# Index units ahead of the convolution units, index dots inside the convolution units, and the 24-row tile of k, q and v on four column groups

## The reference

```python
z = rms_norm(x, g) @ w_in            # 1024 -> q 512, k 512, v 512, ga 512, qi 256, wi 8, ki 32, ub 256, gb 256, cv 256, cg 256, gc 256
q = partial_rope(rms_norm(q per head, q_g)); k = partial_rope(rms_norm(k per head, k_g))     # 8 heads x 64
qi, ki = partial_rope(qi), partial_rope(ki)                                                # 8 index heads x 32
uc = cv * sigmoid(cg)
# A: the keys of each query are chosen by an indexer
sc  = sum_h wi[h] * relu(qi[h] . ki)           # "index dots", masked by position
idx = top_k(sc, L/4);  att = softmax(q . k[idx]) @ v[idx]
# B: causal pooling of ub, windows 2/4/8/16, per-group linear map
# C: depthwise causal convolution of uc, width 31 ("taps"), LayerNorm, swish
y = concat(att * silu(ga), pool * silu(gb), conv * silu(gc));  x = x + y @ w_out
```

## Time and profile before

| | us |
|---|---|
| median of 3 runs (all: 747.38, 752.42, 752.99) | 752.42 |
| profiled execution, its own time | 746.28 |
| its span | 745.0 |
| PE busy | 702.3 (94%) |
| DVE busy | 523.2 (70%) |
| ACT busy | 331.2 (44%) |
| POOL busy | 300.3 (40%) |

### The profile page before, as it was taken

The page is one execution under the profiler, slowest core; times in us unless marked ns, Lnnn a source line. Parts: engine busy times, 40 slices in busy tenths (PEclk is TensorE's granted clock), DMA queues, the critical chain, the costliest instruction groups (busy, mean ns, idle before and its releaser), DMA issues.

```text
span 745.0 us, 13366 instructions
## 1 busy us (share of the span) xinstructions
PE 702.3 (94%) x4690; PEld 567.3 (76%) x4690; DVE 523.2 (70%) x1320; ACT 331.2 (44%) x850; POOL 300.3 (40%) x445
## 2 busy tenths in 40 slices
PE   5899999999889999998999999999988799999998
PEld 5897756578777777776999866666878688777797
DVE  3538888899977977435663898989997777822232
ACT  5525646533947333334132555543485643332212
POOL 1013698942848710011120459895376763000000
PEclk9999999999989999999999999999999899999999
DMA  5543040314232536014025304031522244501203
GB/s 195 160 137 118 17 128 30 114 35 143 58 87 60 179 136 227 1 58 139 21 92 153 126 4 142 30 88 46 157 58 61 83 151 167 170 1 57 96 22 112
DMA packets 54979, 71.90 MB, mean 97 GB/s; under 512 B 12977, under 2 KB 30585, under 8 KB 54881
## 3 DMA queue, kind: packets, MB, share of 16 engines
q1 hardware_dynamic: 54802, 70.96, 30.0%
q10 hardware_dynamic: 111, 0.08, 0.0%
HBM read 64.05 MB, written 7.61 MB: 96 GB/s over the span
## 4 chain that ended last, share of the span: by engine, by line
PE 70%; DVE 21%; ACT 3%; issue 2%; DMA 2%; POOL 1%; SPq 0%; ACTq 0%; DVEq 0%; POOLq 0%
PE R L1273 16%; PE R L1260 6%; PE R L1244 6%; PE R L1262 6%; PE R L1261 6%; PE R L1245 6%; PE R L1246 6%; DVE bias L1715 5%; DVE small L1713 5%; PE R L1409 4%; PE A L1360 3%; PE A L1213 2%; PE A L1438 2%; DVE W_r L1614 2%; PE R L1213 1%
## 5 line engine op out<-in xcount | busy, mean ns | idle before, releaser
L1260 PE MATMUL R<-x_hi,W_r 128*128 128x268 f32 x448 | 137.7, 307 | 5.9 <-DVE bufA L1614 3.3
L1262 PE MATMUL R<-x_hi,W_r 128*128 128x268 f32 x448 | 133.3, 297 | 0.0
L1261 PE MATMUL R<-x_lo,W_r 128*128 128x268 f32 x448 | 133.0, 297 | 0.0
L1244 PE MATMUL R<-W_r,x_hi 128*128 128x512 f32 (+3 forms) x320 | 123.0, 385 | 3.3 <-DVE W_r L1614 3.3
L1273 PE MATMUL R<-yT,W 128*128 128x268 f32 (+2 forms) x768 | 124.2, 318 | 1.0 <-DVE gt L1882 1.0
L1273 PEld LDWEIGHTS R<-yT,W 128*128 128x128 f32 x768 | 106.9, 190 | 16.8 <-issue 6.2
L1245 PE MATMUL R<-W_r,x_hi 128*128 128x512 f32 (+3 forms) x320 | 118.4, 370 | 0.0
L1246 PE MATMUL R<-W_r,x_lo 128*128 128x512 f32 (+3 forms) x320 | 118.1, 369 | 0.0
L823 POOL TENSOR_TENSOR W_r<-W,W_r 128x256 fp32r<-128x256 f32 x112 | 79.4, 742 | 53.1 <-ACT W_r L940 52.3
L1260 PEld LDWEIGHTS R<-x_hi,W_r 128*128 128x128 f32 x448 | 89.5, 200 | 14.5 <-issue 8.5
L1261 PEld LDWEIGHTS R<-x_lo,W_r 128*128 128x128 f32 x448 | 89.9, 201 | 0.0
(11 more groups left out here) (259 smaller groups left out, 1219.7 us busy)
## 6 DMA issues: line engine op xcount, KB each, us to landing
W<-in_w_in SPq DMA_DIRECT2D x52, 512.0 KB, 4.7
KV<-in_cache_k SPq DMA_DIRECT2D x32, 256.0 KB, 3.0
W<-in_w_out SPq DMA_DIRECT2D x8, 1024.0 KB, 6.6
KV<-in_cache_v SPq DMA_DIRECT2D x32, 256.0 KB, 3.9
ubx<-qkv_rows SPq DMA_DIRECT2D x16, 256.0 KB, 3.5
W<-in_w_in SPq DMA_DIRECT2D x8, 296.0 KB, 3.5
out_new_k_prompt<-kz SPq DMA_DIRECT2D x8, 256.0 KB, 2.2
out_new_v_prompt<-V SPq DMA_DIRECT2D x8, 256.0 KB
```

The lines of the kernel that those rows point to most:

```text
L1244: pe.matmul(out, x_hi[:, kc, rows], hi, start=(kc == 0), stop=False)
L1260: pe.matmul(out, hi[:, cols], x_hi[:, kc, toks], start=(kc == 0), stop=False)
L1261: pe.matmul(out, hi[:, cols], x_lo[:, kc, toks], start=False, stop=False)
L1262: m = pe.matmul(out, lo[:, cols], x_hi[:, kc, toks], start=False, stop=(kc == KC - 1))
```

## The change

Five things move or change, in both layers:
- The idx units come first (tiles 1, 2, 0, 3, 4), then the state turns, then the conv units. The idx turns stand behind the first three conv units, and all 40 index dots stand inside the last five conv units, a pair behind every second `kc`. The dots have four PSUM banks instead of two. DVE gathers eight pieces ahead of the evacuation of each of these conv units.
- In the k and q loops of PE no dots are left. DVE's loops hold three taps per tile (four in the last) and two selects per tile.
- Tile 0 of k, q and v is made by `unit_first`: x is put together again for these 24 rows (`x24`, one POOL row), and plain float32 products with both weight parts run on four column groups of 128 output columns, 64 matmuls of 24 x 128 instead of 24 of 24 x 512. ACT evacuates tile 0 in four pieces (k and q: four copies and four squares; v: four copies).
- The weights of the idx units are the ones loaded and split first. For layer 1 the first two of these four loads are split at step "ahead" (four ACT and four DVE rows of 296 columns instead of eight of 256), the other two behind the value products, ahead of the last eight output units (ACT) and between the evacuations of these (DVE).
- Some ACT and DVE weight splits and SP's stores of the index keys move with them.

The diff, cut:

```diff
-EARLY = (CONV_ORDER
-         + [("idx", i, 0) for i in range(NT)]
+IDX_ORDER = (1, 2, 0, 3, 4)
...
             first = slice(XCOL[0], XCOL[0] + ROWS_P[0])
+            x24_s.did(pool.tensor_tensor(x24[:, :, :], x_hi[:, :, first].bitcast(F32), x_lo[:, :, first].bitcast(F32), ALU.add))
...
+                if i == 0:
+                    for j in range(4):
+                        copy(kz[0:r, n % 3, 128 * j:128 * j + 128], R[32 * j:32 * j + r, bank(u), 0:128], rinv[0:r, 0:1])
...
+            for n in range(5):
+                for p in range(8 * n, 8 * n + 8):
+                    relu(p)
...
+            def unit_first(u, name):
+
+                k, g = open_unit(u), G[name]
+                for kc, hi, lo, more in chunks(g):
+                    for w in (hi, lo):
+                        for j in range(4):
+                            m = pe.matmul(R[32 * j:32 * j + ROWS_P[0], k, 0:128], x24[:, kc, :], w[:, 128 * j:128 * j + 128].bitcast(F32),
+                                          start=(kc == 0 and w is hi), stop=(kc == KC - 1 and w is lo), skip_group_check=True)
...
             def unit_fm(u, name, col):
...
+                    if u in DOTS_OF and kc % 2 == 1:
+                        dots(DOTS_OF[u] + kc - 1)
...
+            turns_behind = {("conv", 0, 0): (1, 2), ("conv", 1, 0): (0, 3), ("conv", 0, 1): (4,)}
+            for u in CONV_ORDER:
+                unit_fm(u, ("cv", "cg")[u[1] // 2], 128 * (u[1] % 2))
...
             for i in range(NT):
-                unit_tm(("k", i, 0), "k", 4 * i)
+                if i == 0:
+                    unit_first(("k", 0, 0), "k")
+                else:
+                    unit_tm(("k", i, 0), "k")
                 if i >= 2:
                     kq_turn(i - 2)
...
             for u in CONV_ORDER:
+                if u in DOTS_OF:
+                    for p in range(DOTS_OF[u], DOTS_OF[u] + 8):
+                        gather(p)
...
             for i in range(NT):
-                for x in range(0, IX_K, 2):
-                    gather(p)
-                    gather(p + 1)
-                    p += 2
-                    for _ in range(TAPS_K[i] // 2 if x else (TAPS_K[i] + 1) // 2):
-                        tap(j)
-                        j += 1
+                for x in range(TAPS_K[i]):
+                    tap(j)
+                    j += 1
+                between(2)
                 kq_sum(i)
...
                 if n == SX["ahead"] + 1 and l + 1 < DEPTH:
-                    dve.wait_ge(*next_hi.at(4 * AHEAD))
-                    for m in range(AHEAD):
-                        split_rest(dve, l + 1, m, next_lo)
+                    for n_hi in range(4):
+                        dve.wait_ge(*next_hi.at(n_hi + 1))
+                        split_rest(dve, l + 1, n_hi // 2, n_hi % 2, next_lo)
```

More of the change, by code:

```diff
@@ L416, in first_sync @@
                 x_load(i)
-            first_w(0)
-            first_w(1)
+            for m in range(AHEAD):
+                first_w(m)
             x_load(3)
@@ L708, in sync_layer @@
             row_z.did(sp.dma_start(z_dram, zi[0:8, 0, :]))
+            for m in range(10, 14):
+                w_load(m)
             def k_store(i):
@@ L844, in rotate @@
                 return ta, tb
-            for i in range(NT):
+            for i in IDX_ORDER:
                 r = ROWS_P[i]
@@ L1061, in scalar_layer @@
             for i in range(NT):
[L1062 to L1066, removed]
+                if i in (1, 2):
+                    scale_block(15 + i)
                 kq_evac(NT + i)
@@ L1307, in spread, with x_ready, dots, idx_turn @@
                 stage.did(m)
+            def x_ready(i):
+                if l == 0:
+                    pe.wait_ge(*pre_kept.at(2 * i + 2))
+                elif i == 0:
+                    pe.wait_ge(*xd_s.at(0))
+                elif i < 3:
+                    pe.wait_ge(*res_s.at(3 * KC * i - 9 * KC))
+            def dots(first):
+                if first == 0:
+                    pe.wait_ge(*idxk_s.at(NT))
+                    pe.wait_ge(*row_s.at(3))
+                elif first >= 4:
+                    pe.wait_ge(*acc_s.at(first - 2))
+                for p in (first, first + 1):
+                    i, h, lo, hi = PIECES[p]
+                    b = 32 * (h % 4)
+                    ix_s.did(pe.matmul(A[0:ROWS[i], p % 4, 0:hi - lo], qkT[b:b + 32, h // 4, START[i]:START[i] + ROWS[i]],
+                                       qkT[b:b + 32, 2, lo:hi], start=True, stop=True))
+            def idx_turn(i):
+                n = IDX_NTH[i] - 1
+                pe.wait_ge(*idxz_s.at(n + 1))
+                if n >= 2:
+                    pe.wait_ge(*idxk_s.at(n - 1))
+                for j in range(3):
+                    m = turn(A[:, n % 2, 128 * j:128 * j + ROWS_P[i]], zi[0:ROWS_P[i], i, 128 * j:128 * j + 128], ROWS_P[i])
+                idxt_s.did(m)
+            for i in IDX_ORDER:
+                x_ready(i)
+                if l == 0 and i == 0:
+                    pe.wait_ge(*pre_par_k.at(DEPTH))
+                unit_tm(("idx", i, 0), "idx")
+                if l == 0 and i == 1:
+                    first_params(pe)
+                    first_turn(pe, 3)
+                    first_turn(pe, 4)
+                if l and i == 2:
+                    pe.wait_ge(*sa_s.at(0))
+                    for x in range(NT):
+                        m = pe.matmul(A[0:SR, 3, x:x + 1], row[:, XCOL[x]:XCOL[x] + SR], ones[:, 0:1], start=True, stop=True)
+                    stats_s.did(m)
             pe.wait_ge(*diag_s.at(NT))
```

304 lines of the change are left out of this document (140 added, 164 removed).

## The result

The changed kernel takes **776.81 us** (median; 775.74 to 777.84) against 751.46 of before in the same comparison: ratio 1.0346, interval 1.0301 to 1.0391, 25.4 us slower. The forecast was 767, within 750 to 780. The direction and the place are as forecast; the loss is 25.4 us where 15 were expected. The profiled execution of before (746.28, granted clock 0.984) is one of its short ones, most others lying near 752 at a clock of 0.97 to 0.98, so the two traces differ by 31.6 us where the medians differ by 25.4.

The account below looks back on a forecast made before the run. PE and POOL were taken to bound the k and q units together. 746.3 + 8.7 (layer 0) - 2.0 (splits) + 9.5 (layer 1) = 762.5 us, plus 4.5 for the runs' scale: 767, range 750 to 780.

Parts of the forecast that it names:

- What bounds: In the k and q units, PE and POOL arrive together; POOL's ten tiles and four weight rests take 77.8 us themselves.
- Term 1: Dots moved ahead of k tile 0 start POOL's chain 12.7 us later in layer 0, 13.3 in layer 1.
- Term 2: POOL's chain of ten tiles and four weight rests takes 76.6 us instead of 77.8, ending 11.4 or 12.1 us later.
- Term 3: A tile-0 unit on PE takes 4.0 us, saving 1.8 each, 5.4 per layer; PE waits some 17 us in its turns.
- The clock's share: If the clock drops in PE's waits before the attention loop, the loop starts up to 1.5 us later still.
- Term 4: The attention loop gives back up to 3 us, leaving shifts of 8.7 us in layer 0 and 9.5 in layer 1.
- Term 5: At the weight splits for layer 1, PE's two gaps go: 2.0 us less.
- The sum: Whole kernel, profiled execution's scale: 746.3 + 8.7 - 2.0 + 9.5 = 762.5 us; 767 on the runs' scale.
- the third rival: Tile-0 column groups run one behind another, about 10 us more per layer, 782 to 787 us; chance 0.04.

Follow-up runs that it names:

- before_short_pool: The kernel before, without POOL's multiplication of k and q by their norm gains: 751.77 us, ratio 0.9995.
- short_pool_chain: The changed kernel, without POOL's multiplication of k and q by their norm gains: 751.67 us, ratio 1.0008 to the kernel before.
- columns_alone: The kernel before, with only tile 0 of k, q and v put on four column groups and the order kept: 751.29 us, ratio 0.9999.
- columns_short_pool: The kernel before, with tile 0 on four column groups and without POOL's multiplication by the norm gains: 750.17 us, ratio 0.9958.
- reorder_alone: The changed kernel, with tile 0 of k, q and v made as ordinary units: 775.83 us, ratio 1.0327 to the kernel before.
- dots_in_fours: The changed kernel, with index dots four at a time behind every fourth kc instead of two behind every second: 770.64 us, ratio 1.0249 to the kernel before.

## Why the prediction was right, and what was mis-sized

- **What bounds (PE and POOL arrive together): right.** A shorter POOL chain does nothing before (before_short_pool) and takes 25 us off the changed kernel (short_pool_chain). What I left out is DVE: a PE that is 5.4 us faster in the order of before meets DVE's weight rests and the lower clock, not POOL (columns_alone, columns_short_pool).
- **Term 1 (POOL's chain starts 12.7 and 13.3 us later): the mechanism right, the size short by 3.** It starts 16.0 us later in layer 0, and in layer 1 31.2 - 15.4 = 15.8 behind the layer's own shift. The miss lies ahead of k tile 0; the 9.9 us from there to POOL's first row came out at 9.97, in part by luck: the rows listed for them add up to 10.3 and more, the two selects among these take 0.5 us and not 1.1, and the last gathers start 0.5 us behind k tile 0, which was not counted. Ahead of k tile 0 I priced a pair of dots from its start to the next matmul, 13.1 us in all, and left out what the change costs the 128-row matmuls next to it. PE, changed kernel:

```profile
52.92 0.52 PE L1352 MATMUL A<-qkT 32*128 32x144 f32 x4
53.37 0.39 PE L1305 MATMUL R<-x_hi,W_r 128*128 128x268 f32 x1
53.59 0.28 PE L1306 MATMUL R<-x_lo,W_r 128*128 128x268 f32 x1
...
54.29 0.50 PE L1352 MATMUL A<-qkT 32*128 32x272 f32 x2
```

  Six conv matmuls take 54.29 - 53.37 = 0.92 us between two pairs; at the pace of the earlier trace rows, 0.12 each, they take 0.74. Twenty times 0.18 is 3.6. The waits for DVE, for which I had allowed 0.3, were 0.9, and 0.8 us of waits that PE had ahead of k tile 0 before, at the idx turns, are gone: 3.6 + 0.6 - 0.8 = 3.4, the miss at k tile 0 in layer 1. The trace of before had it too: twelve matmuls of 512 columns between two pairs take 2.98 us, where 12 x 0.23 are 2.79. There it lay beside POOL's chain, as the dots did.

```profile
431.82 0.51 PE L1244 MATMUL R<-W_r,x_hi 128*128 128x512 f32 x1
...
434.80 0.52 PE L1360 MATMUL A<-qkT 32*128 32x144 f32 x4
```

- **Term 2 (76.6 us for the chain): right**, 76.59 and 76.56.
- **Term 3 (a tile-0 unit of 4.0 us; PE waits 17 us): right**, 3.88 and 14.7. The four column groups overlap here: four weight loads start within 0.02 us of each other (85.56 to 85.58), beside matmuls that last 0.27 each. This does not agree with the rule on row groups that I had weighed against it from the Trainium skill ("TensorE: Matmul & The Clock Gate", Part 3: Packing small matmuls). The clock's share (up to 1.5): v tile 1 took 7.21 us behind a wait of 1.96, 1.4 more than a unit at the upper level, so PE reached its last turn 1.45 us behind POOL's end.
- **Term 4 (the loop gives back up to 3): right as far as it goes**, 2.5 by the fourth scores. The blocked DVE row, 3.2 us per layer, is a term that the sum did not have; I had looked for who waits for whom by semaphores, and this wait has none. Half of it, 1.5 us, is the lower clock behind the wait, and that is not certain: in layer 1 of reorder_alone and layer 0 of dots_in_fours the row takes 6.03 and 6.03 us too, and the step from the sixth to the seventh scores takes 11.3 us, against 12.8 in the changed kernel and 9.6 before.
- **Term 5 (-2.0): right**, 2.4; both gaps of the earlier trace rows are gone:

```profile
367.01 1.16 PE L1506 MATMUL A<-pmT,Vm 128*128 128x128 f32 x8
368.00 0.60 PE L1251 MATMUL R<-cst,ksq 128*128 128x128 f32 x4
368.53 1.06 PE L1570 MATMUL A<-KV,pts 128*32 128x512 f32 x8
369.53 0.38 PE L1321 MATMUL R<-yT,W 128*128 128x132 f32 x1
```

- **The sum**: 16.2 us forecast between profiled executions, 31.6 measured. Two times 3.4 of term 1 and two times 3.2 of the blocked row make 13.2 of the 15.4 that are missing; most of the rest is lower clock in layer 0's loop. By medians the loss is 25.4, 10 more than forecast; what the other executions of before do differently from the traced one was not traced. The forecast's own bounds for these terms were 760 to 764 on the scale of the profiled executions, where 777.84 was measured, and the time lies only 3 us inside a range whose upper end was set by where the third rival begins. That it lies inside is in part luck.

## What to carry to other kernels

Before work is moved, look for the engine that is full in that stage, not over the span: 13 us of PE work cost nothing beside a POOL chain of 77 us and cost all of their time ahead of it. When several engines finish a stage within a few us of each other, a saving on one of them buys little, and taking away one bound shows the next at once: here POOL, then DVE's weight rests, then the lower clock behind the waits. And a chain of waits that names one engine at 70% says little of how close the second one is.

## What the runs showed of the hardware

- A DVE row of 64x30 elements took 6.03 us instead of 0.17 when it came 0.6 us later against POOL's rows and ran into eight of them without a gap between; with POOL's rows ordered behind it, it took 0.17 again. Apart from this row, in both layers, no DVE row of that trace took more than 1.31 us, though others fell into such runs of POOL rows.
- A change between 128-row matmuls and 32-row dots costs PE about 0.2 us a pair beyond the dots themselves (0.18 by rows, 0.23 by dots_in_fours, where other waits grew by 0.4 us in all).
- 64 float32 products of 24 rows by 128 columns on four column groups took 3.88 us, 0.06 each, where nothing made them wait.
